# The last stage of a two-block sequence model: products in plain fp32 from the weight ring instead of three rounded products

## The chip, the cores and the metric

The program runs on one core of one Trainium2 chip. The metric is the device time of one execution in microseconds (us). The kernel before took 2109.85 us, the median of two runs (2109.08 and 2110.61 us).

## The reference, cut to what matters

The program computes two transformer-like blocks over 512 tokens of width 1024. Only the end of the second block is touched by the change:

```
y = concat([hyena, gla, gdn], -1) @ w_out              # 1024 -> 1024
x = x + g1 * y
h = modulate(x, norm2_g, sh2, sc2)                     # rms norm, gain, shift
x = x + g2 * (square(relu(h @ w_mlp1)) @ w_mlp2)       # 1024 -> 4096 -> 1024
return rmsnorm(x, final_norm_g)
```

Before `w_out` the outputs of the two recurrent branches (gla and gdn) go through a norm by heads and a gate. Also in this stage one row of the modulation, `g2 = silu(c) @ w_mod`, is computed. All is float32.

## The kernel before, in words

Activations lie transposed: a tensor of 512 tokens and 1024 features is 8 blocks of 128 features (partitions) x 512 tokens. `DB` is 8, `T` is 512, `P` is 128.

**The weight ring.** All large weights are one stream of units of 128x1024 floats (512 KB). The ring in SBUF has 6 slots. SyncE (SP) starts the load of unit u once the count `used` says that unit u-6 is no longer needed; `landed[slot]` counts the arrivals. One unit holds the 8 weight tiles of 128x128 that make one output block of 128 features out of 8 input blocks, so one unit is 8 products.

**Three rounded products.** `product` (lines 240 to 242) multiplies in fp32r, a rounded form of fp32: weights and activations are each split into a rounded part `hi` and a rest `lo = x - hi`, and three matmuls hi·hi, hi·lo, lo·hi are added up in PSUM. For the weights, class `Split` does this: ScalarE (ACT) casts a unit from the ring to `weights_hi` (`round`, line 212), VectorE (DVE) subtracts to `weights_lo` (`rest`, line 216), and with that the ring slot counts as used. Two units of hi and lo are kept, so the cast of unit i waits for the products of unit i-2.

**The last stage**, `stage_tail`, works through 72 units: 8 for `w_out`, then the MLP in two halves of its width, each half 16 units of `w_mlp1` and 16 of `w_mlp2`. All instructions of an engine stand in the order of the code; semaphores join the engines.

- Start: ACT squares the two head tensors (line 3823), DVE sums them (3917), ACT takes roots, DVE inverts and scales (3903, 3905), TensorE (PE) turns them (`turn_heads`, 3762), DVE gates them into blocks 2 to 7 of `src` (3912). Blocks 0 and 1 of `src` are ready from the stage before. ACT and DVE split every block of `src` (3826, 3832, 3899). PE works on unit 0 block by block as they come.
- Output product: unit i gives output block i in PSUM bank i; DVE adds it to `xT` (3934), ACT squares the result for the norm (263), DVE adds the squares (269). Between these, DVE sums the modulation row (3892, 3895), whose weights arrive in `wide_b` by transfers from SP and ACT.
- Middle: the norm (274, 281, 287, 293), the modulation row's sum over partitions (1763), then `h_scaled` (3885), its rounded form with the shift (3848, ACT), its rest (3949, DVE).
- Up products: a unit gives one hidden block. ACT takes relu out of PSUM (3857), GpSimd (POOL) squares (3878), ACT rounds (3860), DVE subtracts the rest (3959).
- Down products: two units per output block in each half; DVE adds the result to `xT` (3967), once in each half.
- End: the final norm, `xT` scaled (3974), eight transfers to memory.

`keep_busy` (line 248) issues small matmuls whose results are unused; they fill the time in which PE would stand still.

Of the kernel before, what the change touches and what calls it, by code (L numbers as in the profile page):

```python
# [13 lines left out]
F32 = mybir.dt.float32  # L14
U32 = mybir.dt.uint32
F32R = mybir.dt.float32r
# [4 lines left out]
P = 128  # L21
D = 1024
DB = D // P
T = 512
# [73 lines left out]
class Core:  # L98
# [3614 lines left out]
def stage_tail(k, src, heads, out_factor, gain, shift, mlp_factor):  # L3713

    HV, N_HEAD = 96, NT * 4
    HB = 16
    U2 = 2 * DB
    N = DB + 2 * (HB + U2)
    with ExitStack() as st:
        w = Split(k, st)  # L3720
        h = [k.rounded(x) for x in (k.B, k.A)]
        hi, lo = (k.sb("mlp_" + x, [P, HB, T], st, F32R) for x in ("hi", "lo"))
        scaled_x = k.sb("h_scaled", [P, 4, T], st)
        relu, hid = scaled_x[:, 0:2, :], scaled_x[:, 2:4, :]
        wm = k.B[:, :, :].rearrange("p (i a) t -> p i (a t)", a=2)
        stat = k.sb("hn_stat", [P, 2, N_HEAD], st)
        early = k.rounded(hi, dt=F32)
        head_sq = [early[:, 8 + 3 * i:11 + 3 * i, :].rearrange("p b t -> p (b t)").rearrange("p (n c) -> p n c", c=HV) for i in range(2)]
# [3 lines left out]
        with k.block() as block:  # L3732
            s_rounded, s_rested, h_scaled, h_rounded, h_rested = (
                k.sig(x) for x in ("src_rounded", "src_rested", "h_scaled", "h_rounded", "h_rested"))
            relu_done, h_done, x_done, rounded, rested = (k.sig(x) for x in ("relu_done", "he_done", "x_done", "rounded", "rested"))
            y_done, stored = k.sig("y_done"), k.sig("stored")

            def unit(half, i):
                return DB + half * (HB + U2) + i
# [17 lines left out]
            def _(pe):  # L3757
# [8 lines left out]
                for i in range(DB):  # L3766
                    w.ready(pe, i)
                    if 1 <= i < 7:
                        pe.wait_ge(hn_gated.sem, hn_gated.at(i))
                    for kt in range(DB):  # L3770
                        if i == 0:
                            if kt in (2, 3):
                                turn_heads(kt - 2)
                                keep_busy(k, pe, 6 if kt == 2 else 4, 7)
                            pe.wait_ge(s_rested.sem, s_rested.at(kt + 1))
                        mm = product(pe, k.ps[:, i, :], w.parts(i, kt * P, (kt + 1) * P), (hi[:, kt, :], lo[:, kt, :]), kt == 0, kt == DB - 1)
                    mm.then_inc(w.done.sem, w.done.up())
# [7 lines left out]
                for half in range(2):  # L3785
                    for i in range(HB):
                        u = unit(half, i)
                        w.ready(pe, u)
                        if u == DB + 6:
                            pe.wait_ge(m_added.sem, m_added.at(1))  # L3790

                        if i >= 8:
                            pe.wait_ge(relu_done.sem, relu_done.at(half * HB + i - 7))
                        elif half:
                            pe.wait_ge(x_done.sem, x_done.at(DB + i + 1))
                        for kt in range(DB):
                            if u == DB:
                                pe.wait_ge(h_rested.sem, h_rested.at(kt + 1))
                            mm = product(pe, k.ps[:, i % 8, :], w.parts(u, kt * P, (kt + 1) * P), (h[0][:, kt, :], h[1][:, kt, :]),
                                         kt == 0, kt == DB - 1)  # L3800
                        mm.then_inc(w.done.sem, w.done.up())
                    for i in range(DB):
                        pe.wait_ge(relu_done.sem, relu_done.at(half * HB + 9 + i))
                        for j in range(2):
                            u = unit(half, HB + 2 * i + j)
                            w.ready(pe, u)
                            for kt in range(8):
                                f = 8 * j + kt
                                if i == 0:
                                    pe.wait_ge(rested.sem, rested.at(half * HB + f + 1))  # L3810
                                mm = product(pe, k.ps[:, i, :], w.parts(u, kt * P, (kt + 1) * P), (hi[:, f, :], lo[:, f, :]), f == 0, f == HB - 1)
                            mm.then_inc(w.done.sem, w.done.up())
# [4 lines left out]
            def _(act):  # L3817
# [6 lines left out]
                w.round(act, 0)  # L3824
                for kt in range(2):
                    act.copy(hi[:, kt, :], src[:, kt, :]).then_inc(s_rounded.sem, s_rounded.up())
                root(0)
                root(1)
                w.round(act, 1)
                for kt in range(2, DB):  # L3830
                    act.wait_ge(hn_gated.sem, hn_gated.at(kt - 1))
                    act.copy(hi[:, kt, :], src[:, kt, :]).then_inc(s_rounded.sem, s_rounded.up())
                for i in range(DB):
                    if i:
                        w.round(act, i + 1)
                        act.wait_ge(x_done.sem, x_done.at(i))
                        norm.square(act, i - 1, k.xT[:, i - 1, :])
# [6 lines left out]
                w.round(act, DB + 1)  # L3844
                act.wait_ge(m_ready.sem, m_ready.at(1))
                for b in range(DB):
                    act.wait_ge(h_scaled.sem, h_scaled.at(b + 1))
                    act.activation(h[0][:, b, :], scaled_x[:, b % 4, :], ACT.Identity, bias=shift(b)).then_inc(h_rounded.sem, h_rounded.up())
                for half in range(2):
                    for i in range(HB):  # L3850
                        if half or i:
                            w.round(act, unit(half, i) + 1)
                        n = half * HB + i
                        w.wait(act, unit(half, i))
                        if n >= 2:
                            act.wait_ge(h_done.sem, h_done.at(n - 1))
                        act.activation(relu[:, n % 2, :], k.ps[:, i % 8, :], ACT.Relu).then_inc(relu_done.sem, relu_done.up())  # L3857
                        act.wait_ge(h_done.sem, h_done.at(n + 1))

                        act.copy(hi[:, i, :], hid[:, n % 2, :]).then_inc(rounded.sem, rounded.up())  # L3860
                    for i in range(U2):
                        if unit(half, HB + i) + 1 < N:
                            w.round(act, unit(half, HB + i) + 1)
                        if half and i % 2 and i > 1:
                            b = i // 2 - 1
                            act.wait_ge(x_done.sem, x_done.at(2 * DB + b + 1))
                            last.square(act, b, k.xT[:, b, :])
                act.wait_ge(x_done.sem, x_done.at(3 * DB))
                last.square(act, DB - 1, k.xT[:, DB - 1, :])
                last.root(act)  # L3870

            @block.gpsimd
# [378 lines left out]
```

## Time and profile before

| | us |
|---|---|
| median of two runs | 2109.85 |
| span of the profiled execution | 2095.9 |
| of it: from the start of the last stage to the end | 443.3 |
| PE busy in the whole span | 1930.3 (92%) |
| PE busy from 1733.7 to 2081.6 | 347.9 of 347.9 |

The span runs from the first to the last instruction of the profiled execution; for that execution no time other than its span is listed. The last stage is read from about 1652.6 us on, where PE's first matmul of it begins. A row of the timeline merges neighbouring instructions of one kind: start, duration, engine, line, operation, output<-inputs, shapes and how many.

### The profile page before, as it was taken

To read this page: it belongs to the slowest core of one execution; us is meant where nothing else is said; L and a number is where in the kernel's file an instruction comes from. 1 tells how busy PE (TensorE), PEld (TensorE's weight loads), DVE (VectorE), ACT (ScalarE), POOL (GpSimd) and SP (SyncE) were. 2 spreads that over 40 slices of the span, in tenths; PEclk is the share of its full clock that TensorE was granted. 3 is DMA by queue.
4 is the path that set the end of the run, shared out by engine and by line. 5 is a ranking of instruction groups with operands and counts; after the bars stand their busy time and mean duration, and the time that the engine had idled before them with its cause. 6 is when DMAs were issued, how large, how long until landed. Compare 5 with 4: busy or idle time off the path is not lost. (4 is left out here: it accounts for less than half of the span.)

```text
span 2095.9 us, 42448 instructions
## 1 busy us (share of the span) xinstructions
PE 1930.3 (92%) x18014; PEld 1432.8 (68%) x18014; DVE 1017.8 (49%) x1836; ACT 633.9 (30%) x1172; POOL 264.8 (13%) x459
## 2 busy tenths in 40 slices
PE   6999999999999869877899998999998899999997
PEld 4776678787748733222678775477787777888886
DVE  6666544434278721110458655465665673333333
ACT  4555432332132212211337331112211333322321
POOL 1000152342100011111000000012322001100100
PEclk9999999999999879999799999999999999999998
DMA  5222100000057899999722102320001242322331
GB/s 197 83 80 66 46 26 13 23 13 13 23 193 243 305 358 410 409 409 405 279 99 64 57 21 90 138 71 23 23 3 63 92 131 81 99 92 91 100 100 41
DMA packets 73985, 265.82 MB, mean 127 GB/s; under 512 B 10966, under 2 KB 11478, under 8 KB 72784
## 3 DMA queue, kind: packets, MB, share of 16 engines
q1 hardware_dynamic: 60848, 225.69, 29.5%
q10 hardware_dynamic: 7488, 25.95, 3.5%
q0 software_dynamic: 5472, 11.59, 1.5%
q8 instruction: 138, 2.26, 0.5%
q14 instruction: 39, 0.32, 0.0%
HBM read 254.57 MB, written 17.30 MB: 130 GB/s over the span
## 5 line engine op out<-in xcount | busy, mean ns | idle before, releaser
L216 DVE TENSOR_TENSOR weights_lo<-ring,weights_hi 128x1024 fp32r<-128x1024 f32 x140 | 173.3, 1239 | 146.1 <-ACT weights_hi L212 146.1
L212 ACT CAST weights_hi<-ring 128x1024 fp32r<-128x1024 f32 x140 | 146.1, 1045 | 258.2 <-PE ps L242 254.5
L241 PE MATMUL ps<-wide_b_round,weights_hi 128*128 128x512 f32 (+1 forms) x384 | 141.2, 368 | 0.0
L240 PE MATMUL ps<-wide_b_round,weights_hi 128*128 128x512 f32 (+1 forms) x360 | 131.1, 364 | 2.1 <-DVE wide_a_round L3949 2.1
L242 PE MATMUL ps<-wide_b_round,weights_lo 128*128 128x512 f32 (+1 forms) x360 | 130.3, 362 | 0.0
L240 PE MATMUL ps<-mlp_hi,weights_hi 128*128 128x512 f32 x320 | 125.7, 393 | 4.1 <-DVE mlp_lo L3899 4.1
L241 PE MATMUL ps<-mlp_lo,weights_hi 128*128 128x512 f32 x320 | 125.0, 391 | 0.0
L242 PE MATMUL ps<-mlp_hi,weights_lo 128*128 128x512 f32 x320 | 125.0, 391 | 0.0
L241 PE MATMUL ps<-wide_a_round,weights_hi 128*128 128x512 f32 x256 | 101.2, 395 | 0.0
L240 PE MATMUL ps<-wide_a_round,weights_hi 128*128 128x512 f32 x216 | 92.9, 430 | 3.7 <-DVE wide_b_round L663 3.7
L991 PE MATMUL ps<-wide_a,ring 128*128 128x256 f32 x320 | 87.6, 398 | 0.7 <-issue 0.7
L242 PE MATMUL ps<-wide_a_round,weights_lo 128*128 128x512 f32 x216 | 86.0, 398 | 0.0
L241 PEld LDWEIGHTS ps<-wide_b_round,weights_hi 128*128 128x128 f32 x384 | 72.9, 190 | 17.0 <-issue 1.9
L240 PE MATMUL ps<-hm_hi,weights_hi 128*128 128x512 f32 x200 | 82.4, 412 | 2.0 <-DVE hm_lo L2763 2.0
L240 PEld LDWEIGHTS ps<-wide_b_round,weights_hi 128*128 128x128 f32 x360 | 67.6, 188 | 21.2 <-DVE wide_a_round L3949 5.0
L241 PE MATMUL ps<-hm_lo,weights_hi 128*128 128x512 f32 x200 | 78.7, 393 | 0.0
L242 PE MATMUL ps<-hm_hi,weights_lo 128*128 128x512 f32 x200 | 78.3, 391 | 0.0
L2283 DVE TENSOR_TENSOR sp_he<-sp_silu,ps 128x256 f32<-128x256 f32 x16 | 6.7, 422 | 147.2 <-ACT sp_silu L2170 147.2
L3959 DVE TENSOR_TENSOR mlp_lo<-h_scaled,mlp_hi 128x512 fp32r<-128x512 f32 x32 | 22.2, 695 | 111.8 <-ACT mlp_hi L3860 111.8
L242 PEld LDWEIGHTS ps<-wide_b_round,weights_lo 128*128 128x128 f32 x360 | 67.9, 189 | 11.6
L3878 POOL TENSOR_TENSOR h_scaled<-h_scaled 128x512 f32<-128x512 f32 x32 | 33.4, 1043 | 332.3 <-ACT h_scaled L3857 332.3
L240 PEld LDWEIGHTS ps<-mlp_hi,weights_hi 128*128 128x128 f32 x320 | 60.3, 188 | 18.3 <-DVE mlp_lo L3899 3.1
(625 smaller groups left out, 4057.5 us busy)
## 6 DMA issues: line engine op xcount, KB each, us to landing
ring<-stream_in SPq DMA_DIRECT2D x210, 512.0 KB, 3.5
moe_ring<-stream_in SPq DMA_DIRECT2D x112, 512.0 KB, 13.4
w_mod<-w_mod_in ACTq DMA_DIRECT2D x40, 512.0 KB, 6.5
wide_b<-stream_in SPq DMA_DIRECT2D x32, 512.0 KB
xT<-w_mod_in SPq DMA_DIRECT2D x16, 512.0 KB, 4.3
na_rel<-rel_in POOLq DMA_DIRECT2D x4, 640.0 KB, 6.2
mod_acc<-mod_part ACTq DMA_DIRECT2D x5, 512.0 KB, 6.2
ring<-mod_acc SPq DMA_DIRECT2D x1, 2560.0 KB, 18.5
```

The costliest lines, as they stand in the source:

```text
L212: act.copy(self.hi[:, i % self.n, :], w).then_inc(self.cast.sem, self.cast.up())
L216: ins = eng.tensor_tensor(self.lo[:, i % self.n, :], self.unit(i)[0], self.hi[:, i % self.n, :], ALU.subtract)
L240: pe.matmul(out, left[0], right[0], start=start, stop=False, **kw)
L241: pe.matmul(out, left[0], right[1], start=False, stop=False, **kw)
L242: return pe.matmul(out, left[1], right[0], start=False, stop=stop, **kw)
L991: mm = pe.matmul(k.ps[:, 2 + u % 2, at:at + 256], w, k.A[:, kt, at:at + 256], start=s == 0, stop=s + 2 >= STEPS, skip_group_check=True)
L2283: dve.tensor_tensor(he[:, j % 2, :], sgs[:, j % 2, :], k.ps[:, 0, 256:512], ALU.mult).then_inc(h_done.sem, 1)
L3878: pool.tensor_tensor(hid[:, n % 2, :], relu[:, n % 2, :], relu[:, n % 2, :], ALU.mult).then_inc(h_done.sem, h_done.up())
L3959: dve.tensor_tensor(lo[:, i, :], hid[:, n % 2, :], hi[:, i, :], ALU.subtract).then_inc(rested.sem, rested.up())
```

## The change

In the last stage the split into hi and lo goes, for weights and activations. Every product is one matmul in plain fp32 that reads its weights from the ring slot (`k.unit` waits for the arrival) and its activations from fp32 tiles. PE itself counts the ring slot as used, after the last product of the unit. The MLP is worked in one piece: 32 up units, then 32 down units, four for each output block; so the hidden tile is 32 blocks of fp32 (it takes the room of the rounded and the rest tile), `xT` gets the MLP's result once instead of twice, and the weights are laid out for this order. The square of relu moves from POOL to DVE, in place. The order of the start changes with it: the turns of the two head tensors no longer have a product between them, and the gates no longer have splits between them.

```diff
+    def unit(self, pe):
+        w, landed, full = self.take()
+        pe.wait_ge(landed, full)
+        return w
...
-    HB = 16
-    U2 = 2 * DB
-    N = DB + 2 * (HB + U2)
+    HB = 32
+    PER = HB // DB
+    N = DB + 2 * HB
...
-        w = Split(k, st)
-        h = [k.rounded(x) for x in (k.B, k.A)]
-        hi, lo = (k.sb("mlp_" + x, [P, HB, T], st, F32R) for x in ("hi", "lo"))
-        scaled_x = k.sb("h_scaled", [P, 4, T], st)
+        h = k.B
+        hid = k.sb("mlp_hidden", [P, HB, T], st)
...   (PE, output product)
-                        mm = product(pe, k.ps[:, i, :], w.parts(i, kt * P, (kt + 1) * P), (hi[:, kt, :], lo[:, kt, :]), kt == 0, kt == DB - 1)
-                    mm.then_inc(w.done.sem, w.done.up())
+                        if (i, kt) == (0, 2):
+                            turn_heads(0)
+                            keep_busy(k, pe, 6, 7)
+                            turn_heads(1)
+                            keep_busy(k, pe, 4, 7)
+                        if i == 0 and kt >= 2:
+                            pe.wait_ge(hn_gated.sem, hn_gated.at(kt - 1))
+                        mm = pe.matmul(k.ps[:, i, :], w[:, kt * P:(kt + 1) * P], src[:, kt, :], start=kt == 0, stop=kt == DB - 1)
+                    mm.then_inc(k.used, 1)
...   (PE, MLP)
+                for i in range(HB):
+                    w = k.unit(pe)
+                    if i >= 8:
+                        pe.wait_ge(relu_done.sem, relu_done.at(i - 7))
+                    for kt in range(DB):
+                        if i == 0:
+                            pe.wait_ge(h_ready.sem, h_ready.at(kt + 1))
+                        mm = pe.matmul(k.ps[:, i % 8, :], w[:, kt * P:(kt + 1) * P], h[:, kt, :], start=kt == 0, stop=kt == DB - 1)
+                    mm.then_inc(k.used, 1)
+                for i in range(DB):
+                    pe.wait_ge(relu_done.sem, relu_done.at(HB - 7 + i))
+                    for j in range(PER):
+                        w = k.unit(pe)
+                        for kt in range(8):
+                            f = 8 * j + kt
+                            if i == 0:
+                                pe.wait_ge(hid_done.sem, hid_done.at(f + 1))
+                            mm = pe.matmul(k.ps[:, i, :], w[:, kt * P:(kt + 1) * P], hid[:, f, :], start=f == 0, stop=f == HB - 1)
+                        mm.then_inc(k.used, 1)
...   (ACT; all calls of w.round and the copies to hi are gone)
+                    act.activation(h[:, b, :], h[:, b, :], ACT.Identity, bias=shift(b)).then_inc(h_ready.sem, h_ready.up())
+                for i in range(HB):
+                    act.wait_ge(k.used, k.after(DB + i))
+                    act.activation(hid[:, i, :], k.ps[:, i % 8, :], ACT.Relu).then_inc(relu_done.sem, relu_done.up())
...   (POOL has no work left)
...   (DVE; all calls of w.rest and rest_src are gone)
+                for i in range(HB):
+                    dve.wait_ge(relu_done.sem, relu_done.at(i + 1))
+                    dve.tensor_tensor(hid[:, i, :], hid[:, i, :], hid[:, i, :], ALU.mult).then_inc(hid_done.sem, hid_done.up())
+                for b in range(DB):
+                    dve.wait_ge(k.used, k.after(DB + HB + PER * b + PER - 1))
+                    dve.scalar_tensor_tensor(k.xT[:, b, :], k.ps[:, b, :], mlp_factor(b), k.xT[:, b, :], ALU.mult, ALU.add).then_inc(x_done.sem, x_done.up())
```

PE at the start of the last stage, before (L248 are the small filler matmuls, L240 to L242 one product, L3762 the turns of a head tensor; `mlp_hi` and `mlp_lo` hold the split `src`):

```order
L248 MATMUL ps<-const 128x128 x30
L240 MATMUL ps<-mlp_hi,weights_hi 128x512
L241 MATMUL ps<-mlp_lo,weights_hi 128x512
L242 MATMUL ps<-mlp_hi,weights_lo 128x512
...
L3762 MATMUL ps<-const,wide_a 128x128 x12
L248 MATMUL ps<-const 128x128 x6
L240 MATMUL ps<-mlp_hi,weights_hi 128x512
L241 MATMUL ps<-mlp_lo,weights_hi 128x512
L242 MATMUL ps<-mlp_hi,weights_lo 128x512
L3762 MATMUL ps<-const,gdn_y 128x128 x12
L248 MATMUL ps<-const 128x128 x4
```

And PE of the changed kernel from the same place to its end (every line below line 180 is 5 higher; L3774 is the output product, L3792 up, L3802 down):

```order
L253 MATMUL ps<-const 128x128 x30
L3774 MATMUL ps<-wide_a,ring 128x512 x2
L3758 MATMUL ps<-const,wide_a 128x128 x12
L253 MATMUL ps<-const 128x128 x6
L3758 MATMUL ps<-const,gdn_y 128x128 x12
L253 MATMUL ps<-const 128x128 x4
L3774 MATMUL ps<-wide_a,ring 128x512 x62
...
L253 MATMUL ps<-const 128x128 x9
L3792 MATMUL ps<-wide_b,ring 128x512 x256
L3802 MATMUL ps<-mlp_hidden,ring 128x512 x256
```

Two products now stand ahead of the first turn, none between the turns, and 62 + 256 + 256 behind; with the first two that is 576 plain matmuls, where 3 x 576 rounded ones stood.

DVE at the same place, before (L3917 sums the squares, L3903 and L3905 scale the heads, L3899 is the rest of `src`, L216 the rest of a weight unit, L3912 the gates, L3934 the first addition to `xT`):

```order
L3917 TENSOR_REDUCE hn_stat<-mlp_hi_round_17654 128x16 x2
L216 TENSOR_TENSOR weights_lo<-ring,weights_hi 128x1024
L3903 RECIPROCAL hn_stat<-hn_stat 128x16
L3905 TENSOR_TENSOR wide_a<-wide_a,hn_stat 128x1536
L3899 TENSOR_TENSOR mlp_lo<-wide_a,mlp_hi 128x512 x2
L3903 RECIPROCAL hn_stat<-hn_stat 128x16
L3905 TENSOR_TENSOR gdn_y<-gdn_y,hn_stat 128x1536
L3912 SCALAR_TENSOR_TENSOR wide_a<-ps,cols,gla_gate 128x512 x3
L3899 TENSOR_TENSOR mlp_lo<-wide_a,mlp_hi 128x512
L3912 SCALAR_TENSOR_TENSOR wide_a<-ps,cols,gdn_gate 128x512
```

And now:

```order
L3870 TENSOR_REDUCE hn_stat<-mlp_hidden 128x16 x2
L3856 RECIPROCAL hn_stat<-hn_stat 128x16
L3858 TENSOR_TENSOR wide_a<-wide_a,hn_stat 128x1536
L3856 RECIPROCAL hn_stat<-hn_stat 128x16
L3858 TENSOR_TENSOR gdn_y<-gdn_y,hn_stat 128x1536
L3865 SCALAR_TENSOR_TENSOR wide_a<-ps,cols,gla_gate 128x512 x3
L3865 SCALAR_TENSOR_TENSOR wide_a<-ps,cols,gdn_gate 128x512 x3
L3878 SCALAR_TENSOR_TENSOR xT<-ps,mod,xT 128x512
```

The scaling of the second head tensor follows directly on that of the first, and the six gates follow one another.

## Rows read from the trace of the kernel before

**Rows 1.** The page, busy time of each engine, whole span.

```profile
PE 1930.3 (92%) x18014; PEld 1432.8 (68%) x18014; DVE 1017.8 (49%) x1836; ACT 633.9 (30%) x1172; POOL 264.8 (13%) x459
```

**Rows 2.** Busy time (PE, PEld, DVE, ACT, POOL) by stretch, granted clock, DMA share, GB/s.

```profile
1652.60:1676.90 24.30, 20.16 (x129) 17.09 (x129) 18.56 (x22) 11.09 (x15) 0.00 (x0) 0.93 0.50 195
...
1733.70:2081.60 347.90, 347.90 (x1514) 283.76 (x1512) 112.05 (x114) 104.58 (x133) 33.37 (x32) 1.00 0.26 85
```

**Rows 3.** Timeline of DVE: second and last addition of the output product to xT.

```profile
1682.67 0.75 DVE L3934 SCALAR_TENSOR_TENSOR xT<-ps,mod,xT 128x512 f32<-128x512 f32 x1 [1.79 <-PE ps L242]
...
1715.32 0.75 DVE L3934 SCALAR_TENSOR_TENSOR xT<-ps,mod,xT 128x512 f32<-128x512 f32 x1 [1.77 <-PE ps L242]
```

**Rows 4.** Timeline of ACT: first and last of 16 relus, first half.

```profile
1733.98 0.60 ACT L3857 ACTIVATE h_scaled<-ps 128x512 f32<-128x512 f32 x1 [1.84 <-PE ps L242]
...
1817.97 0.60 ACT L3857 ACTIVATE h_scaled<-ps 128x512 f32<-128x512 f32 x1 [2.28 <-PE ps L242]
```

**Rows 5.** Timeline of DVE: additions of down products, first, eighth, sixteenth.

```profile
1828.88 0.75 DVE L3967 SCALAR_TENSOR_TENSOR xT<-ps,mod,xT 128x512 f32<-128x512 f32 x1 [3.08 <-PE ps L242]
...
1905.04 0.75 DVE L3967 SCALAR_TENSOR_TENSOR xT<-ps,mod,xT 128x512 f32<-128x512 f32 x1 [3.08 <-PE ps L242]
...
2081.71 0.75 DVE L3967 SCALAR_TENSOR_TENSOR xT<-ps,mod,xT 128x512 f32<-128x512 f32 x1 [8.39 <-PE ps L242]
```

**Rows 6.** Timeline of PE: runs of plain fp32 matmuls, 512 and 256 columns.

```profile
610.23 13.90 PE L1523 MATMUL ps<-wide_a,ring 128*128 128x512 f32 x32
...
1309.56 27.63 PE L2923 MATMUL ps<-xT,hy_dft 128*128 128x512 f32 x64
1337.91 13.97 PE L2894 MATMUL ps<-hy_inv,hy_Y 128*128 128x512 f32 x32 [0.72 <-issue]
...
1358.65 17.05 PE L2870 MATMUL ps<-hy_vt,hy_dft 128*128 128x256 f32 x64 [0.68 <-ACT hy_vt L2949]
```

**Rows 7.** Busy time of PE in the run of line 1523, granted clock.

```profile
610.20:623.60 13.40, 13.40 (x35) 1.00 0.37 130
```

**Rows 8.** All matmuls of lines 1523 and 2870: duration min/median/max, ns.

```profile
L1523 PE MATMUL ps<-wide_a,ring x96: 592/592/1061, 575.8 to 623.5; 128*128 128x512 f32 x96
...
L2870 PE MATMUL ps<-hy_vt,hy_dft x128: 379/379/792, 1287.2 to 1375.3; 128*128 128x256 f32 x128
```

**Rows 9.** Timelines of PE, DVE and ACT at the start of the stage.

```profile
1652.68 6.94 PE L248 MATMUL ps<-const 128*128 128x128 f32 x60 [2.44 <-PEq L3084]
1661.85 0.77 PE L240 MATMUL ps<-mlp_hi,weights_hi 128*128 128x512 f32 x1 [2.23 <-DVE mlp_lo L3899]
...
1669.05 1.47 PE L3762 MATMUL ps<-const,gdn_y 128*128 128x128 f32 x12
...
1676.89 0.50 PE L240 MATMUL ps<-mlp_hi,weights_hi 128*128 128x512 f32 x1
...
1654.18 3.41 DVE L3917 TENSOR_REDUCE hn_stat<-mlp_hi_round 128x16 f32<-128x1536 f32 x2 [1.82 <-ACT mlp_hi_round L3823]
...
1659.34 1.76 DVE L3905 TENSOR_TENSOR wide_a<-wide_a,hn_stat 128x1536 f32<-128x1536 f32 x1
...
1654.05 1.47 ACT L3823 ACTIVATE mlp_hi_round<-gdn_y 128x1536 f32<-128x1536 f32 x1
...
1657.51 1.28 ACT L3820 ACT_TABLE_LOAD   x1
```

**Rows 10.** Timelines of PE, DVE and ACT in the middle of the stage.

```profile
1724.27 0.47 PE L240 MATMUL ps<-wide_b_round,weights_hi 128*128 128x512 f32 x1
...
1721.77 1.41 DVE L3885 SCALAR_TENSOR_TENSOR h_scaled<-xT,gain,ps 128x512 f32<-128x512 f32 x2 [1.29 <-PE ps L293]
...
1724.70 0.75 DVE L3949 SCALAR_TENSOR_TENSOR wide_a_round<-h_scaled,mod,wide_b_round 128x512 fp32r<-128x512 f32 x1
...
1724.82 0.72 ACT L3848 ACTIVATE wide_b_round<-h_scaled,mod 128x512 fp32r<-128x512 f32 x1 [0.87 <-DVE h_scaled L3885]
```

**Rows 11.** The page's DMA issues: KB each, us from issue to landing.

```profile
ring<-stream_in SPq DMA_DIRECT2D x210, 512.0 KB, 3.5
```

More of the change, by code:

```diff
@@ L3784, in _ @@
                 keep_busy(k, pe, 9, 0)
[L3785 to L3812, printed above, removed]
@@ new lines, in _ @@
+                for i in range(DB):
+                    pe.wait_ge(relu_done.sem, relu_done.at(HB - 7 + i))
+                    for j in range(PER):
+                        w = k.unit(pe)
+                        for kt in range(8):
[4 more added lines that the diff above has]
+                        mm.then_inc(k.used, 1)
@@ L3847, in _ @@
                     act.wait_ge(h_scaled.sem, h_scaled.at(b + 1))
[L3848 to L3867, printed above, removed]
@@ L3868, in _ @@
-                act.wait_ge(x_done.sem, x_done.at(3 * DB))
-                last.square(act, DB - 1, k.xT[:, DB - 1, :])
-                last.root(act)
-            @block.gpsimd
-            def _(pool):
-                for n in range(2 * HB):
-                    pool.wait_ge(relu_done.sem, relu_done.at(n + 1))
-                    if n >= 2:
-                        pool.wait_ge(rested.sem, rested.at(n - 1))
-                    pool.tensor_tensor(hid[:, n % 2, :], relu[:, n % 2, :], relu[:, n % 2, :], ALU.mult).then_inc(h_done.sem, h_done.up())
+                    act.activation(h[:, b, :], h[:, b, :], ACT.Identity, bias=shift(b)).then_inc(h_ready.sem, h_ready.up())
@@ L3880, in _ @@
+                for i in range(HB):
+                    act.wait_ge(k.used, k.after(DB + i))
+                    act.activation(hid[:, i, :], k.ps[:, i % 8, :], ACT.Relu).then_inc(relu_done.sem, relu_done.up())
+                for b in range(DB):
+                    act.wait_ge(x_done.sem, x_done.at(DB + b + 1))
+                    last.square(act, b, k.xT[:, b, :])
+                last.root(act)
             @block.vector
@@ L3917, in _ @@
                     dve.tensor_reduce(stat[:, i, :], head_sq[i], AX.X, ALU.add).then_inc(hn_summed.sem, hn_summed.up())
-                w.rest(dve, 0)
                 scale_heads(0)
-                rest_src(0)
-                rest_src(1)
                 scale_heads(1)
-                for b in range(2, 5):
+                for b in range(2, DB):
                     gate_heads(b)
-                for b in range(2, 5):
-                    rest_src(b)
-                    gate_heads(b + 3)
-                for b in range(5, DB):
-                    rest_src(b)
                 dve.wait_ge(back.sem, back.at(16))
                 for i in range(DB):
-                    w.rest(dve, i + 1)
-                    w.wait(dve, i)
+                    dve.wait_ge(k.used, k.after(i))
                     dve.scalar_tensor_tensor(k.xT[:, i, :], k.ps[:, i, :], out_factor(i), k.xT[:, i, :], ALU.mult, ALU.add).then_inc(x_done.sem, x_done.up())
@@ L3951, in _ @@
                 a = COL["b_mod"][0] + 5 * DB
                 dve.tensor_tensor(k.mod[:, 40:48, 0], k.ps[:, 6, 0:8], k.cols[:, a:a + 8], ALU.add).then_inc(m_added.sem, m_added.up())
-                for half in range(2):
-                    for i in range(HB):
-                        if half or i:
-                            w.rest(dve, unit(half, i) + 1)
-                        n = half * HB + i
-                        dve.wait_ge(rounded.sem, rounded.at(n + 1))
-                        dve.tensor_tensor(lo[:, i, :], hid[:, n % 2, :], hi[:, i, :], ALU.subtract).then_inc(rested.sem, rested.up())
-                    for i in range(U2):
-                        if unit(half, HB + i) + 1 < N:
-                            w.rest(dve, unit(half, HB + i) + 1)
-                        if i % 2:
-                            b = i // 2
-                            w.wait(dve, unit(half, HB + i))
-                            dve.wait_ge(x_done.sem, x_done.at(DB * (half + 1) + b))
-                            dve.scalar_tensor_tensor(k.xT[:, b, :], k.ps[:, b, :], mlp_factor(b), k.xT[:, b, :], ALU.mult, ALU.add).then_inc(x_done.sem, x_done.up())
-                            if half and b > 1:
-                                last.add(dve, b - 1)
```

51 lines of the change are left out of this document (12 added, 39 removed).

## The prediction, made before the changed kernel ran

> **What bounds the kernel now.** I read the page first: PE is busy for 92% of the span, the next engine for 49% [rows 1]. That share is a mean, so I cut the last stage into stretches. In the longest of them, from the end of the first up unit to the end of the last down unit, PE is busy for all of 347.9 us at the full granted clock, while DVE has work for 112 and ACT for 105 us [rows 2]. The chain of waits says the same: it runs through matmuls of lines 240 to 242 there and nothing else. So in this stretch only PE's own pace counts; what ACT, DVE and POOL do lies beside it and is worth nothing when removed.
>
> The pace itself cannot be taken from the duration of a matmul (about 390 ns), since matmuls overlap; it has to come from repetition. The relus of one half follow the up units: 15 units in 1817.97 - 1733.98 = 83.99 us, 5.60 us a unit [rows 4], so a product of three rounded matmuls costs 0.700 us. The additions of the down products come every (1905.04 - 1828.88) / 7 = 10.88 us for two units [rows 5], 0.680 us a product. The output product goes at (1715.32 - 1682.67) / 6 = 5.44 us a unit [rows 3], 0.680 again.
>
> **The price of a plain fp32 product.** The kernel has such products elsewhere. Line 1523 is the closest: weights from the ring, 512 columns of `wide_a`, 8 products a unit, 6 units. That is 48 instructions and the trace has 96 records [rows 8], so one plain fp32 matmul shows as two. Its last run of 32 records lasts 13.90 us [rows 6]; less the last record's own 0.592 us [rows 8] and divided by the 31 starts between, a record takes 0.4293 us, a product 0.8586 us. Line 2923 gives (27.63 - 0.59) / 63 = 0.4292, line 2894 (13.97 - 0.59) / 31 = 0.4316 [rows 6]. The granted clock was the full one there [rows 7], as in the stretch that is to be replaced [rows 2]. So I take 0.8586 us, with 0.863 as the upper bound. For the lower one: a rounded matmul passes the array once with 512 columns in 0.2267 us at best, and no row shows a plain product in less than 0.858; I allow 0.853.
>
> That is the heart of the change: 0.8586 in place of 0.680 or 0.700, on the engine that bounds the stage, 576 times.
>
> A rule speaks for a still higher price. The Trainium skill, page "FP8 and Floating Point Precision", section "TensorE Precision Notes", says that true FP32 takes four passes through the array. With each pass at the pace of a rounded matmul here a product would cost 4/3 of the present one, 0.907 to 0.933 us; the trace's own plain products come out 5 to 8% below that. I go by the trace and keep the other value as a rival.
>
> **The change part by part**, by the times of the profiled execution:
>
> *Start, to the first product of output unit 1; before at 1676.89 [rows 9].* PE's fillers end at 1659.6 (1652.68 + 6.94). Then it stood 2.23 us for the rest of `src` and worked unit 0 in pieces between splits. Now the first two products need only a landed unit (ACT cast it right after its squares, so it is there): 2 x 0.86, to 1661.3. The turn of heads 0 needs the first scaling. ACT's table load no longer stands behind a cast and two copies; it can begin at 1655.5 after the squares, 1.28 us long, so the first root is out by 1657.1, but DVE is in its sums until 1657.6. Reciprocal (some 0.25) and scaling (1.76 [rows 9]) end at 1659.6, those of the second at 1661.6. So PE does not wait: turns 1.4 us (12 records in 1.47 [rows 9]), 6 fillers 1.4 and 4 fillers 0.9 (60 records in 6.94, two a filler [rows 9]), turns again 1.4, to 1666.4. The gates are DVE passes over 128x512 like that of 0.75 us [rows 10], ahead of PE at 0.86. Six products more give 1671.5. That is 5.4 us earlier. Should the granted clock fall here for some microseconds, as it does now (0.93 over the stretch [rows 2]), up to 2 us of it go; I take **-5.0**, between -3 and -6.
>
> *Output units 1 to 7.* Before 1676.89 to 1715.32, 38.4 us; now 56 x 0.8586 = 48.1: **+9.7**. DVE fitted addition, square sum, modulation sum and a weight rest into 5.44 us; now it has 6.87 for the first three. Its wait is now on the ring count, which PE raises at the same moment as `products_done` before; what is queued behind it is the same less the weight rests.
>
> *Middle, 1715.3 to 1724.3.* Norm, modulation sum, spread and fillers stand in PE's order as before, and the weight rest that left DVE's order here was covered by the spread (to 1721.8). The first scaled block starts behind the spread at 1721.77, ACT's shift takes 0.72, so block 0 is ready by about 1723.3, while PE's fillers last until the first up product at 1724.27 [rows 10]: the first up product starts as late as before, **0**.
>
> *Up unit 0.* Before, DVE made scaled and rest block in turn (each pass 0.75 [rows 10], overlapping a little, so some 1.3 us a block), and PE followed that: 1733.98 - 1724.27 = 9.7 us [rows 4, 10]. Now DVE gives a block in one pass and ACT one every 0.72 [rows 10], faster than PE's 0.86: 8 x 0.8586 = 6.87, **-2.8**.
>
> *The other 31 up and the 32 down units.* Before 2081.71 - 1733.98 = 347.7 us [rows 4, 5] for 504 products; now 504 x 0.8586 = 432.7: **+85.0**. Nothing else can step in: per unit of 6.87 us ACT has one relu (0.6), DVE one square (about 0.7), the eight banks are left long before they are written again, and at the turn from up to down PE needs hidden block 31 only 31 products in. A unit lands in 3.5 us [rows 11] and five are ahead of PE, although a slot is now given back after its products and not after DVE's subtraction; 512 KB in 6.87 us is 76 GB/s, less than the 85 of today [rows 2].
>
> *Removed at no gain:* 72 casts and 72 rests of weights, the splits of the hidden blocks, POOL's squares, eight additions to `xT`: all under PE's cover, except where named above. *End, from the last addition:* unchanged, 0.
>
> Sum: -5.0 + 9.7 - 2.8 + 85.0 = **+86.9 us**. The profiled span is 2095.9, so a span of 2182.8. The median of the two runs lies 13.95 us above the span (no time beside the span is listed for the profiled execution); nothing in the change touches what lies there. 2109.85 + 86.9 = 2196.8, say **2197 us**, 4.1% slower.
>
> **Rivals.**
>
> 1. *Each record of a plain product takes as long as two rounded matmuls.* From 0.680 and 0.700 us [rows 3 to 5] that is 0.907 us for 312 products and 0.933 for 248, the rest alike: 312 x 0.048 + 248 x 0.075 + 1 = 35 us more, **2232 us**. For it: the 20 ns that a rounded matmul takes above 512 columns at 2.4 GHz could be a cost of this stage. Against: line 1523 reads from the same ring and the same `wide_a` and shows 0.8586. 4%.
> 2. *Weight loads come out from under the matmuls.* With 256 columns a plain record takes (17.05 - 0.38) / 63 = 0.265 us [rows 6, 8], 0.050 more than half of 0.4293. If that load time showed at 512 columns in a long run, 2 x 0.050 x 576 = 58 us more, **2255 us**. The Trainium skill, "TensorE: Matmul & The Clock Gate", section "Weight-path perf modes", says that its fast weight load is not used for FP32. Against: the rows with 512 columns already hold their loads. 3%.
> 3. *The other side: two passes, not slower.* If each of the two records of a plain product ran at a rounded matmul's pace, 0.453 to 0.467 us a product, the stage would lose 230 us against my forecast, **1967 us**. The place is PE's stream from 1671 to the end; it decides from the price at which the sum is zero, 0.8586 - 86.9 / 576 = 0.708 us; below 0.63 the kernel is faster by over 2%. For it: two records a product where three stood. Against: the start-to-start time of every plain run. 2%, and 2% for a price between 0.64 and 0.78, about 2130.
> 4. *The ring runs dry,* since slots are returned later: needs a landing over 34 us; 1%, above 2210.
>
> **How the numbers follow.** The forecast has 88%. Its own spread: price 0.853 to 0.863 gives -3 and +3; the start +2 and -1; the middle's clock ±2; one execution against another some 5. Together 2187 to 2208, and that holds over 8 in 10, so the rivals stay outside. Within 2% (42 us, about what a measurement of this kernel can tell from no change) only the middle price of rival 3: 2%. Faster: 2%. Slower: 96%.
>
> **What would show it.** Up and down additions in the changed trace: the relus 6.87 us apart, additions of the down products 27.5 us apart (four units), output additions 6.87. PE at full clock and busy throughout, DVE and ACT nearly idle. First product of output unit 1 near 1671.5, first up product 9.0 us behind the last output addition, up unit 0 in 6.9. 1152 records in the stage's products. A record pace other than 0.429 us would make the prediction wrong by 1.15 us for each nanosecond of it; gaps in PE between units would speak for rival 4.

## The result and the profile after

The changed kernel takes 2190.38 us (median of two runs, 2187.10 and 2193.65), 1.040 times the kernel before, with a 95% interval of 1.033 to 1.047. In the first experiment below the same kernel was timed again: 1.043, interval 1.039 to 1.047. The forecast was 2197 us and 4.1% slower.

The profiled execution has a span of 2185.3 us and a time of 2187.10, so 1.8 us lie outside the span. This distance is 1.8 us, give or take 0.1, in every run here. Its last stage begins 3.3 us later than that of the profile before, though nothing ahead of it was changed. I therefore compare the last stage alone, from PE's first filler matmul to the end of the span: 443.2 us before (2095.9 - 1652.68) and 529.3 after (2185.3 - 1655.96), 86.1 us more.

The page of the changed kernel: busy time of the engines, and the two groups that hold the MLP's products (line, engine, operation, operands, count; busy time, mean ns).

```profile
PE 2025.4 (93%) x17438; PEld 1330.7 (61%) x17438; DVE 913.5 (42%) x1740; ACT 538.2 (25%) x1060; POOL 229.8 (11%) x427
...
L3792 PE MATMUL ps<-wide_b,ring 128*128 128x512 f32 x512 | 219.9, 592 | 0.0
L3802 PE MATMUL ps<-mlp_hidden,ring 128*128 128x512 f32 x512 | 219.9, 592 | 0.0
```

DVE, ACT and POOL together lost 235 us of work against [rows 1], and the kernel is slower. The two groups show why: 2 x 512 records, no idle time before them, 440 us of PE time for 512 products.

The timeline of PE gives the pace of the long runs; the busy times by stretch are those of the stage's start, of output units 1 to 7, of the middle, and of the rest (columns as in [rows 2]).

```profile
1734.51 216.89 PE L3792 MATMUL ps<-wide_b,ring 128*128 128x512 f32 x505
1951.24 219.90 PE L3802 MATMUL ps<-mlp_hidden,ring 128*128 128x512 f32 x512
```

```profile
1655.90:1676.15 20.25, 20.19 (x121) 16.27 (x122) 11.38 (x12) 4.57 (x5) 0.00 (x0) 0.92 0.54 208
1676.15:1724.15 48.00, 48.00 (x114) 21.29 (x113) 17.37 (x20) 4.42 (x7) 0.00 (x0) 1.00 0.37 121
1724.15:1731.50 7.35, 6.89 (x66) 6.51 (x65) 4.80 (x7) 1.87 (x4) 0.00 (x0) 1.00 0.25 74
...
1738.60:2171.20 432.60, 432.53 (x1008) 191.14 (x1006) 30.38 (x45) 23.49 (x39) 0.00 (x0) 1.00 0.22 71
```

(219.90 - 0.592) / 511 = 0.4292 us a record, 0.8583 us a product. The row of the up products lacks the first 7 of its 512 records, since the view began behind them; (216.89 - 0.592) / 504 is 0.4292 too. What bounds the stage is what bounded it before, PE, now with ACT at 23 and DVE at 30 of 432.6 us. The rows that answer to [rows 3 to 5], from the timelines of DVE and ACT (output and down additions on DVE, then relus on ACT):

```profile
1676.15 0.75 DVE L3878 SCALAR_TENSOR_TENSOR xT<-ps,mod,xT 128x512 f32<-128x512 f32 x1 [3.98 <-PE ps L3774]
...
1724.15 0.75 DVE L3878 SCALAR_TENSOR_TENSOR xT<-ps,mod,xT 128x512 f32<-128x512 f32 x1 [4.32 <-PE ps L3774]
...
1978.91 0.75 DVE L3896 SCALAR_TENSOR_TENSOR xT<-ps,mod,xT 128x512 f32<-128x512 f32 x1 [26.15 <-PE ps L3802]
...
2171.17 0.75 DVE L3896 SCALAR_TENSOR_TENSOR xT<-ps,mod,xT 128x512 f32<-128x512 f32 x1 [26.12 <-PE ps L3802]
```

```profile
1738.57 0.60 ACT L3833 ACTIVATE mlp_hidden<-ps 128x512 f32<-128x512 f32 x1 [2.77 <-PE ps L3792]
...
1951.44 0.60 ACT L3833 ACTIVATE mlp_hidden<-ps 128x512 f32<-128x512 f32 x1 [6.27 <-PE ps L3792]
```

The waits at the end of these rows grew from 2.3 us (last relu of the first half) and 3.1 us (down additions) to 6.3 and 26 us: the engines beside PE stand still most of the time. 31 units from the first relu to the last take 212.87 us (6.87 each), seven steps of four units 192.26 (27.47 each).

### The profile page after: what moved, and what is told of

It is laid out like the page before. It is cut to its first block and busy times, and to the rows that moved or that the text cites. A ratio compares the mean times of both kernels' runs of the same rounds, so it can differ in the third digit from the quotient of the medians.

```text
span 2185.3 us, 40902 instructions
## 1 busy us (share of the span) xinstructions
PE 2025.4 (93%) x17438; PEld 1330.7 (61%) x17438; DVE 913.5 (42%) x1740; ACT 538.2 (25%) x1060; POOL 229.8 (11%) x427
## 5 line engine op out<-in xcount | busy, mean ns | idle before, releaser
L3792 PE MATMUL ps<-wide_b,ring 128*128 128x512 f32 x512 | 219.9, 592 | 0.0
L3802 PE MATMUL ps<-mlp_hidden,ring 128*128 128x512 f32 x512 | 219.9, 592 | 0.0
L3802 PEld LDWEIGHTS ps<-mlp_hidden,ring 128*128 128x128 f32 x512 | 97.3, 190 | 122.5 <-issue 122.5
L3792 PEld LDWEIGHTS ps<-wide_b,ring 128*128 128x128 f32 x512 | 97.2, 190 | 122.0 <-issue 121.0
L246 PE MATMUL ps<-wide_b_round,weights_hi 128*128 128x512 f32 (+1 forms) x384 | 139.9, 364 | 0.0
L221 DVE TENSOR_TENSOR weights_lo<-ring,weights_hi 128x1024 fp32r<-128x1024 f32 x68 | 85.0, 1253 | 75.2 <-ACT weights_hi L217 75.2
L217 ACT CAST weights_hi<-ring 128x1024 fp32r<-128x1024 f32 x68 | 70.7, 1044 | 107.4 <-PE ps L247 103.8
L245 PE MATMUL ps<-wide_a_round,weights_hi 128*128 128x512 f32 x216 | 92.3, 427 | 3.7 <-DVE wide_b_round L668 3.7
L246 PEld LDWEIGHTS ps<-wide_b_round,weights_hi 128*128 128x128 f32 x384 | 72.1, 188 | 16.7 <-issue 1.9
L253 PE MATMUL ps<-const 128*128 128x128 f32 x454 | 66.5, 304 | 6.2 <-PEq L2430 3.5
```

The lines of the kernel that those rows point to most:

```text
L217: act.copy(self.hi[:, i % self.n, :], w).then_inc(self.cast.sem, self.cast.up())
L221: ins = eng.tensor_tensor(self.lo[:, i % self.n, :], self.unit(i)[0], self.hi[:, i % self.n, :], ALU.subtract)
L245: pe.matmul(out, left[0], right[0], start=start, stop=False, **kw)
L246: pe.matmul(out, left[0], right[1], start=False, stop=False, **kw)
L253: pe.matmul(k.ps[:, bank, 0:P], k.c("ident"), k.c("ones"), start=True, stop=True)
L3792: mm = pe.matmul(k.ps[:, i % 8, :], w[:, kt * P:(kt + 1) * P], h[:, kt, :], start=kt == 0, stop=kt == DB - 1)
```

## Experiments

All are cut at the same marks of the last stage, in us: **start** (PE's first filler to the first output addition), **output** (first to eighth addition), **middle** (eighth addition to the first relu), **rest** (first relu to the last addition), **end**.

| kernel | start | output | middle | rest | end | stage |
|---|---|---|---|---|---|---|
| before | 24.3 | 38.4 | 18.7 | 347.7 | 14.2 | 443.2 |
| after | 20.2 | 48.0 | 14.4 | 432.6 | 14.1 | 529.3 |
| after_again | 18.8 | 48.0 | 14.4 | 432.6 | 14.2 | 528.0 |
| out_plain | 18.8 | 48.0 | 18.3 | 347.7 | 14.2 | 447.0 |
| two_plain | 18.8 | 38.0 | 15.7 | 347.6 | 14.4 | 434.5 |
| late_slot | 18.8 | 48.0 | 14.4 | 432.6 | 14.1 | 527.9 |
| four_rounded | 23.0 | 38.4 | 18.0 | 463.6 | 14.2 | 557.2 |
| up_256 | 18.8 | 48.0 | 14.5 | 433.8 | 14.1 | 529.2 |
| up_256_apart | 18.8 | 48.0 | 15.9 | 433.8 | 13.6 | 530.1 |
| square_dve | 24.2 | 38.4 | 18.7 | 347.7 | 14.2 | 443.2 |
| swap_h | 23.1 | 38.4 | 17.8 | 347.7 | 14.4 | 441.4 |
| weights_last | 23.0 | 38.4 | 17.7 | 347.7 | 13.3 | 440.2 |

**The changed kernel again** (no edit).

> The changed kernel once more, timed in three rounds beside the kernel before. Theory (the price of a plain product, 0.8583 us, decides): the last stage, from PE's first filler to the end, takes 529.3 us as in the first profile, against 443.2 before, so +86 us; what comes ahead of the stage varies by a few us from one execution to another and belongs to neither kernel. Ratio of the times 1.041. Rival (the clock decides part of it): the stage itself varies by more than 3 us between the two profiles of the same kernel.

Ratio 1.043 (1.039 to 1.047). Four runs lie between 2183.25 and 2197.41 us, 21 runs of the kernel before between 2093.78 and 2115.79: whole times differ by 1% between executions of one kernel. The stage differs by 1.4 us between the two profiles, and all of that is in the start. Theory held. The 1.4 us are the granted clock. First the changed kernel's first profile, then this run: PE's first 60 filler records, and the granted clock (third number from the end) of short windows.

```profile
1655.96 8.36 PE L253 MATMUL ps<-const 128*128 128x128 f32 x60 [2.44 <-PEq L3089]
```

```profile
1656.00:1658.00 2.00, 2.00 (x9) 0.50 0.72 139
1658.00:1660.00 2.00, 2.00 (x16) 0.76 0.88 369
1660.00:1662.00 2.00, 2.00 (x20) 1.00 1.02 426
```

```profile
1667.15 6.94 PE L253 MATMUL ps<-const 128*128 128x128 f32 x60 [2.44 <-PEq L3089]
```

```profile
1667.00:1669.00 2.00, 1.84 (x16) 1.00 0.63 139
1669.00:1671.00 2.00, 2.00 (x20) 1.00 0.85 344
```

With the same work ahead of it (2.44 us without a matmul in both), PE got 1.2 GHz for some 3 us in one execution and 2.4 GHz in the other. In both PE had the full clock up to the 2.44 us in which it stood still; in the first the clock fell then, in the second it did not.

**Only the output product plain.**

```diff
-    mm = product(pe, k.ps[:, i, :], w.parts(...), (hi[:, kt, :], lo[:, kt, :]), kt == 0, kt == DB - 1)
+    mm = pe.matmul(k.ps[:, i, :], wi[:, kt * P:(kt + 1) * P], src[:, kt, :], start=kt == 0, stop=kt == DB - 1)
```

with the start in the changed order, and the MLP as before; its first two weight units are split at the end of the output product.

> Only the output product is plain fp32 from the ring, with the changed order of the start; the MLP is as before, in three rounded products and two halves. Theory: the parts add up. Start to the end of output unit 0: 20.2 us (before 24.2); units 1 to 7: 7 x 6.87 = 48.1 (before 38.4); middle 7.4 to 9.0 according to the granted clock; up unit 0 9.7 and everything behind it as before. Stage 443.2 - 4.0 + 9.7 = 448.9 us, 447.3 if the clock stays up in the middle. Rival (the start gained because the splits of the whole stage were gone, not by its own order): start 24 us, stage 453.

Ratio 1.003 (0.9997 to 1.006); stage 447.0, expected 447.3 with a full clock. The start is as short as in the changed kernel (18.8) and the output as long (48.0), while the rest (347.7) is that of before, and so is the middle to half a microsecond (18.3 against 17.7 to 18.7 us in before, square_dve, swap_h and weights_last). Timeline of DVE, first and eighth output addition:

```profile
1682.30 0.75 DVE L3928 SCALAR_TENSOR_TENSOR xT<-ps,mod,xT 128x512 f32<-128x512 f32 x1 [3.98 <-PE ps L3786]
...
1730.30 0.75 DVE L3928 SCALAR_TENSOR_TENSOR xT<-ps,mod,xT 128x512 f32<-128x512 f32 x1 [4.32 <-PE ps L3786]
```

The parts add up; the start's gain comes from what was changed in the start itself, not from the missing splits of the MLP. Two things changed there, the order of the work and the missing splits of `src` and of the output weights, and no run separates them.

**Plain only where PE waited for splits.** Of the kernel before, output unit 0 and the first up unit are plain; the splits of `src` and `h` run under them. `h` exists once more, as plain fp32, in blocks of `mlp_hi` that are still free. PE counts the ring slots.

```diff
+    if i == 0:
+        mm = pe.matmul(k.ps[:, i, :], wi[:, kt * P:(kt + 1) * P], src[:, kt, :], start=kt == 0, stop=kt == DB - 1)
+        continue
+    if i == 1:
+        pe.wait_ge(s_rested.sem, s_rested.at(kt + 1))
...
+    if u == DB:
+        pe.wait_ge(h_ready.sem, h_ready.at(kt + 1))
+        mm = pe.matmul(k.ps[:, i % 8, :], wi[:, kt * P:(kt + 1) * P], h_plain[:, kt, :], start=kt == 0, stop=kt == DB - 1)
+        continue
```

> Only output unit 0 and the first up unit are plain fp32 products; the other 70 units are three rounded ones. Ring slots are given back by PE after the products. Theory: the two places where PE waits for splits are covered by plain products, the rest keeps the rounded pace. Start -4.0, first up unit -2.7, output units 1 to 7 5.44 us each and the 63 last units 347.7 us as before: stage 443.2 - 6.7 = 436.5 us, faster than both kernels, ratio 0.997. Rival (the splits only come later, and output unit 1 or up unit 1 then waits for them instead): stage 440 to 445 us, no gain.

Ratio 0.997 (0.994 to 0.999), median 2095.63 us of twelve runs against 2105.68 of the 21 beside them. The interval leaves out 1, but 0.3% is far below the 2% from which a time counts here as another; what shows the gain is the stage, 434.5 us against 440.2 to 443.2 in those same four profiles, where all products of the stage are three rounded ones. That is 8.7 us less than in the profile before. Expected were 6.7, and the 2.1 us that stretches of half clock cost in that profile (see the section on the prediction) make up the rest. PE's timeline shows the plain first up unit (16 records, 8 products) and rounded products right behind it, with no wait:

```profile
1721.72 7.03 PE L3849 MATMUL ps<-mlp_hi_round,ring 128*128 128x512 f32 x16
1728.19 0.80 PE L282 MATMUL ps<-wide_b_round,weights_hi 128*128 128x512 f32 x1
```

**Ring slots given back late.**

```diff
-                sp.wait_ge(self.used, u - RING + 1)
+                sp.wait_ge(self.used, u - RING + 1 + (4 if u >= STREAM["out2"][0] + RING + 2 else 0))
```

> The changed kernel, but in the last stage SP starts the load of a unit only when the unit two ahead of it in the stream is used up, so that one unit instead of five is ahead of PE. Theory (the loads are hidden, a landing of 3.5 us against 6.87 us a unit): no wait, the relus stay 6.87 us apart, stage 529 us. Rival (the later return of the slots is a cost that the loads nearly fill): PE waits for landings; with a landing above 6.87 us each unit is longer by what exceeds it, 62 us for each us of it.

Stage 527.9, rest 432.6: no wait. The loads of the MLP's time, with KB and median us to landing, and first and last relu:

```profile
ring<-stream_in SPq DMA_DIRECT2D x61, 512.0 KB, 3.4
```

```profile
1737.81 0.60 ACT L3833 ACTIVATE mlp_hidden<-ps 128x512 f32<-128x512 f32 x1 [2.76 <-PE ps L3792]
...
1950.67 0.60 ACT L3833 ACTIVATE mlp_hidden<-ps 128x512 f32<-128x512 f32 x1 [6.27 <-PE ps L3792]
```

31 units in 212.86 us with one unit ahead instead of five. Rival 4 of the prediction is out with room to spare.

**Four rounded products in the MLP.**

```diff
+    if four:
+        pe.matmul(out, left[1], right[1], start=False, stop=False, **kw)
```

> The kernel before, with the fourth rounded product lo x lo added in the MLP's 512 products (not in the output product). Theory (a plain product streams its columns four times, but loads weights only twice and pays the overhead of a start only twice): four rounded matmuls cost more than one plain product, 4 x 0.2267 = 0.907 us down and 4 x 0.2333 = 0.933 up, so the stage is 443 + 256 x 0.2267 + 248 x 0.2333 = 559 us, 30 more than with plain products. Rival (four passes cost the same in either form): 0.858 us a product, stage 443 + 504 x 0.168 = 528 us.

Stage 557.2 (expected 559). The rest takes 463.6 us for 504 products, 0.920 us each against 0.858 for a plain one. First and sixteenth relu: 112.0 us for 15 up units, 0.933 a product.

```profile
1735.79 0.60 ACT L3859 ACTIVATE h_scaled<-ps 128x512 f32<-128x512 f32 x1 [2.12 <-PE ps L244]
...
1847.79 0.60 ACT L3859 ACTIVATE h_scaled<-ps 128x512 f32<-128x512 f32 x1 [4.15 <-PE ps L244]
```

This is what rival 1 of the prediction would have cost, now as a real kernel: four separate rounded matmuls are 7% dearer than one plain one.

**Up products in two halves of 256 columns,** on the same weights one after the other. In this kernel the sums of the two halves alternate in one bank, and what it leaves there is not the up product; its work on PE is the same. The next kernel, which finishes one half before it begins the other, computes the whole function.

```diff
-    mm = pe.matmul(k.ps[:, i % 8, :], w[:, kt * P:(kt + 1) * P], h[:, kt, :], ...)
+    for c in range(2):
+        cs = slice(c * 256, (c + 1) * 256)
+        mm = pe.matmul(k.ps[:, i % 8, cs], w[:, kt * P:(kt + 1) * P], h[:, kt, cs], ...)
```

> The changed kernel, with each up product as two matmuls of 256 columns on the same weights, so the same columns are streamed and weights are loaded twice as often. Theory (with 512 columns the loads are hidden, with 256 they are not): 0.265 us a record, 4 x 0.265 = 1.06 us a product, an up unit 8.5 us, stage 529 + 256 x 0.2 = 580 us. Rival (only the columns count): up unit 6.9 us, stage 529 to 532.

My theory failed. 15 up units took 103.60 us, 6.907 each; 0.2158 us a record instead of 0.265. Twice as many weight loads cost 0.04 us a unit. The rival held: only the columns count.

**The halves apart,** so that neighbours have different weights.

```diff
-                        for kt in range(DB):
+                    for c in range(2):
+                        cs = slice(c * 256, (c + 1) * 256)
+                        for kt in range(DB):
```

> The changed kernel; each up unit now goes twice over its 8 weight tiles, first with the left 256 columns, then with the right ones. So each matmul of 256 columns meets other weights than the one ahead of it. In the run up_256, where two neighbours had the same weights, a record took 0.2158 us and not the 0.265 of line 2870. Theory same (a load is only hidden behind 256 columns when it brings the same weights): 0.265 us a record, an up unit 8.5 us, stage 580 us. Rival place (what line 2870 pays comes from where its operands lie or from its own stage, not from new weights): 6.9 us a unit, stage 529.

Again the rival: 6.907 us a unit. First and sixteenth relu, and the count of matmul records of the up products (ns min/median/max):

```profile
1736.74 0.60 ACT L3836 ACTIVATE mlp_hidden<-ps 128x512 f32<-128x512 f32 x1 [4.24 <-PE ps L3794]
...
1840.34 0.60 ACT L3836 ACTIVATE mlp_hidden<-ps 128x512 f32<-128x512 f32 x1 [6.31 <-PE ps L3794]
```

```profile
L3794 PE MATMUL ps<-wide_b,ring x1024: 379/379/483, 1728.2 to 1950.4; 128*128 128x256 f32 x171
```

So the loads lie under even half as long matmuls here, with new weights each time. The 0.265 us of line 2870 [rows 6], from which both theories and rival 2 of the prediction took their price, is no cost of a load either. It is the granted clock. Of that run in the kernel before, the timeline of PE for 1359 to 1364 and for 1365 to 1375 us, and the granted clock (third number from the end) of both parts:

```profile
1358.65 5.91 PE L2870 MATMUL ps<-hy_vt,hy_dft 128*128 128x256 f32 x13 [0.68 <-ACT hy_vt L2949]
1364.74 10.52 PE L2870 MATMUL ps<-hy_vt,hy_dft 128*128 128x256 f32 x48
```

```profile
1358.70:1364.60 5.90, 5.90 (x14) 0.50 0.01 6
1364.80:1375.40 10.60, 10.60 (x51) 1.00 0.30 99
```

The first records stand 0.427 us apart ((5.91 - 0.792) / 12, the longest duration of [rows 8] for the last one), at 1.2 GHz; the later ones (10.52 - 0.379) / 47 = 0.2158 us apart at 2.4 GHz, the pace of up_256 to the digit. 0.265 is the mean of the two.

**Why up products took 0.700 us and down products 0.680.** Three edits of the kernel before: POOL's squares moved to DVE; the two parts of `h` exchanged between their tiles; the weight tiles placed behind the activation tiles.

```diff
-                    pool.tensor_tensor(hid[:, n % 2, :], relu[:, n % 2, :], relu[:, n % 2, :], ALU.mult).then_inc(h_done.sem, h_done.up())
+                        dve.tensor_tensor(hid[:, n % 2, :], relu[:, n % 2, :], relu[:, n % 2, :], ALU.mult).then_inc(h_done.sem, h_done.up())
...
-        h = [k.rounded(x) for x in (k.B, k.A)]
+        h = [k.rounded(x) for x in (k.A, k.B)]
...
-        w = Split(k, st)
         scaled_x = k.sb("h_scaled", [P, 4, T], st)
+        w = Split(k, st)
```

> The kernel before, with the squares of relu on DVE instead of POOL. Question: why up products take 0.700 us and down and output products 0.680 before. Theory POOL (its squares beside the matmuls take SBUF time from PE): up units go to 5.44 us, stage 438 us. Rival (the place or pairing of the activation tiles decides, POOL has no part): up units stay at 5.60 us, stage 443.

> The kernel before, with the rounded part of h in wide_a and its rest in wide_b, the other way round. POOL is out as the reason why an up product takes 0.700 us and a down product 0.680. Theory pairing (which tile holds which part decides): up units change from 5.60 to 5.44 us, or to another value. Rival (both tiles' places as a pair, or something else of the up phase): 5.60 us stays, stage 443.

> The kernel before, with the tiles weights_hi and weights_lo placed behind the activation tiles in SBUF instead of ahead of them; no instruction changes. Theory place (the distance of weights and activations in SBUF decides how much of the load shows behind 512 columns): the pace of the up, down or output units changes from 5.60, 5.44 and 5.44 us. Rival: all three stay, stage 443.

None of the three moved the pace. First and sixteenth relu of square_dve, then of weights_last, 84.00 us apart in both, as in [rows 4]:

```profile
1737.26 0.60 ACT L3857 ACTIVATE h_scaled<-ps 128x512 f32<-128x512 f32 x1 [1.84 <-PE ps L242]
...
1821.26 0.60 ACT L3857 ACTIVATE h_scaled<-ps 128x512 f32<-128x512 f32 x1 [2.67 <-PE ps L242]
```

```profile
1739.60 0.60 ACT L3857 ACTIVATE h_scaled<-ps 128x512 f32<-128x512 f32 x1 [1.84 <-PE ps L242]
...
1823.60 0.60 ACT L3857 ACTIVATE h_scaled<-ps 128x512 f32<-128x512 f32 x1 [2.28 <-PE ps L242]
```

The cause of these 0.020 us is not found; other places of `h` itself were not tried. It is worth 5 us of the kernel before and nothing to the changed one, whose three paces are alike.

## Why the prediction was right, step by step

- **PE bounds the stage, and its pace is to be read from repetition.** Held. The work removed from the other engines gave nothing outside the two places named.
- **The price, 0.8586 us.** Measured 0.8583 in all three kinds of product, with weights from the ring and three different activation tiles. A row of another stage was the right thing to read it from, since operation, shape, weight source and granted clock agreed.
- **Start, -5.0 us (between -3 and -6).** -4.1 in the first profile, -5.5 in the runs where the clock stayed up: the sum had -5.4 for that case. The split of the two cases is the 1.4 us of slow fillers shown above. Part of the gain is not the change's: in the profile before, the first two products of unit 0 and the turn behind them ran at half the granted clock (0.50 from 1661.8 to 1665.0 us). In weights_last and swap_h, with the same instructions and the full clock there, the start takes 23.0 and 23.1 us instead of 24.3. So some 4.3 us are the change's own.
- **Output units, +9.7; up unit 0, -2.8; the 63 units behind, +85.0.** Measured +9.6 (the first of the seven steps is 6.80 us, the other six are 6.87), -2.6 (7.07 us from 1731.50 to 1738.57 against 9.7) and +84.9.
- **Middle, 0.** Mis-sized: it was 1.6 us shorter, 7.35 us from the last output addition to the first up product against 8.95, within the ±2 us that the prediction gave the clock there. The order of work is the same. PE's spread (L293, now L298) and the fillers behind it lost it; the timeline of the kernel before, then of the changed one, then of weights_last:

```profile
1719.68 2.05 PE L293 MATMUL ps<-rms_r,const 128*128 128x128 f32 x8
1721.53 2.93 PE L248 MATMUL ps<-const 128*128 128x128 f32 x18
```

```profile
1728.52 1.14 PE L298 MATMUL ps<-rms_r,const 128*128 128x128 f32 x8
1729.49 2.17 PE L253 MATMUL ps<-const 128*128 128x128 f32 x18
```

```profile
1726.22 1.14 PE L293 MATMUL ps<-rms_r,const 128*128 128x128 f32 x8
1727.19 3.80 PE L248 MATMUL ps<-const 128*128 128x128 f32 x18
```

  Before, PE had half the granted clock there for some 3 us (0.50 from 1720 to 1723). What such a stretch costs depends on what it falls on. In before and square_dve it held back the spread, for which DVE waits with `h_scaled`, and the middle of the table takes 18.7 us. In swap_h there was none, and it takes 17.8. In weights_last it came a microsecond later, on fillers alone, and it takes 17.7: PE made up for it, since the products of up unit 0 follow DVE's rests anyway. So 0.9 us of the profile before are the clock's. And in swap_h the first up product starts 8.0 us behind the last addition, after a wait of 0.5 us for the rest of `h`, a wait that the changed kernel does not have: the prediction's reason for 0, that the fillers set this start, held only because they were slow.
- **The time.** The stage came out 86.1 us longer against a sum of 86.9. Between swap_h and after_again, where no slow stretch cost anything at the start or in the middle, it is 86.5. What was wrong is the anchor: I took the 13.95 us between the profiled span and the median of two runs for time outside the span. Outside lie 1.8 us; the other 12 were the difference between one execution and another. Adding the sum to the median was still the right thing to do, since it does not need the split, but the ±5 us I gave for one execution against another was small: 21 runs of one kernel spread over 22 us, and a single run of the changed kernel took 2183.25, below the range. That the first median lies 7 us from the forecast is in part luck.
- **The rule of four passes.** The Trainium skill's four passes ("FP8 and Floating Point Precision", section "TensorE Precision Notes") fit this trace, two to a record. A plain record of 512 columns takes 0.4292 us, twice 512 columns at 2.4 GHz (426.7 ns) and 2.5 ns. What I set beside it was wrong, a pass at the pace of a rounded matmul, for that pays 13 to 20 ns over its columns each time: 226.7 and 233.3 ns against 213.3. The Trainium skill, "TensorE: Matmul & The Clock Gate", section "Back-to-back issue gap", gives N / 2.4 + 2.5 ns for a matmul on its own; with N the columns of both passes of a record, the plain records here agree with it (0.4292 and, with 256 columns, 0.2158 us), though they stand in a long run; the rounded ones do not.
- **Rival 2, weight loads.** It misread its row. The 0.265 us a record of line 2870 [rows 6] is a mean over a stretch at half clock and one at full clock, as shown behind up_256_apart; at the full clock it is 0.2158, which leaves nothing to come out from under a matmul. The prediction looked up the clock for line 1523 [rows 7] and not for this row.
- **Rival 3's second price.** A price between 0.64 and 0.78 us gives 2071 to 2152 us by the prediction's own sum, 2111 in the middle and not 2130. Nothing else hung on it.

## What to carry to other kernels

A product of three fp32r matmuls costs 0.68 to 0.70 us here, one plain fp32 matmul 0.858, four fp32r matmuls 0.907 to 0.933: where PE is the bound, splits on idle engines are worth their work, and where PE stands waiting for a split, a plain product is the cheaper filler. So the two can be mixed, plain for the first unit after fresh activations and rounded behind it; that was worth some 7 us of this stage. And price a swapped instruction from rows of the same operation and shape elsewhere in the program, by start-to-start time in a long run, with the granted clock of that very run beside it: line 2870 shows what happens without.

## What the runs showed of the hardware

- At the same place of the same work, PE's clock is granted in full or at half from one execution to another. At the start of the stage it was at half for some 3 us during the first fillers in after and four_rounded, for some 6 us in swap_h, and for some 3 us about 9 us later in before and square_dve; not at all in the other seven profiles. In the middle it was at half for some 3 us in before, square_dve and weights_last, not in the other nine.
- What that costs depends on what waits for the slowed work: 1.4 us in after; 1.2 us at the start and 0.9 us in the middle of before; nothing in weights_last, nor in swap_h, where the 60 filler records took 9.81 us instead of 6.94 but the next product would have waited for DVE anyway (2.23 us in before [rows 9]).
- At the full clock a plain fp32 record costs 2.5 ns over its columns (each streamed twice) with 512 and with 256 columns, in the last stage and in line 2870 alike, although a weight load of 190 ns belongs to each; a rounded matmul with 512 columns and the same load costs 13 or 20 ns over them. What tells these apart is open.
